# Score products of attention at full array height: a head's high and low query parts stacked in the two row halves

## What is computed

```python
qg = q.reshape(b, T, KV, G, HEAD_DIM)                      # 2 groups of 4 heads
s = jnp.einsum('bcqkgd,bcskd->bckgqs', qc, kw) * SCALE     # window: keys of this and the two chunks before
s = jnp.einsum('bqkgd,bqskd->bqkgs', qg, kg) * SCALE       # sparse: of all earlier keys, the top 256
```

## Time and profile before

| what | us |
|---|---|
| median of 3 runs | 1798.72 (1798.32 to 1801.7) |
| the profiled execution, its own time | 1803.05 |
| span of its instructions | 1801.2 |
| PE busy in the span | 1750.7 (97%) |
| DVE busy | 1257.2 (70%) |
| ACT busy | 726.3 (40%) |
| POOL busy | 588.0 (33%) |

### The profile page before, as it was taken

How to read it: one execution, slowest core, us unless ns; L and a number is a source line. 1 busy time by engine, 2 the same in 40 slices (tenths; PEclk the granted TensorE clock), 3 DMA queues, 4 the chain that set the end, 5 groups by cost and what they waited for, 6 DMA issues and landing times.

```text
span 1801.2 us, 32125 instructions
## 1 busy us (share of the span) xinstructions
PE 1750.7 (97%) x12267; PEld 1700.1 (94%) x12267; DVE 1257.2 (70%) x2174; ACT 726.3 (40%) x1274; POOL 588.0 (33%) x477
## 2 busy tenths in 40 slices
PE   5999999999999999899999999999999999999998
PEld 5999999989999998778889999999999999999998
DVE  5367868978787876688747348866666666776765
ACT  5342122258811123777752335333333333422334
POOL 2211212256634332422231000654555545121030
PEclk9999999999999999999999999999999999999999
DMA  4111111110111112311123210222222222542212
GB/s 147 53 26 52 36 36 53 47 29 25 42 41 52 41 39 78 77 46 38 49 64 116 81 46 26 94 84 72 83 84 72 84 72 75 193 133 81 93 36 97
DMA packets 180435, 121.21 MB, mean 67 GB/s; under 512 B 9340, under 2 KB 165260, under 8 KB 180300
## 3 DMA queue, kind: packets, MB, share of 16 engines
q1 hardware_dynamic: 179324, 117.37, 21.6%
q0 software_dynamic: 976, 2.00, 0.4%
HBM read 101.45 MB, written 17.89 MB: 66 GB/s over the span
## 4 chain that ended last, share of the span: by engine, by line
PE 89%; DVE 5%; ACT 2%; issue 1%; DMA 1%; POOL 1%; SPq 0%; DVEq 0%; ACTq 0%; POOLq 0%
PE ps L1341 36%; PE ps L1711 22%; PE ps L1784 7%; PE ps L1770 6%; PE ps L1353 4%; PE ps L1491 3%; PE ps L1468 3%; PE ps L1606 2%; PE ps L1566 2%; DVE probs L2773 1%; PE ps L1371 1%; DMA w_raw_in_lo<-in_w_in 0%; DMA x_rows<-in_x_prompt 0%; PE ps L1432 0%; PE ps L1433 0%
## 5 line engine op out<-in xcount | busy, mean ns | idle before, releaser
L1079 POOL TENSOR_TENSOR w_lo<-w_raw,w_hi 128x1024 fp32r<-128x1024 f32 (+1 forms) x53 | 100.6, 1897 | 341.6 <-ACT w_hi L1872 341.6
L1341 PE MATMUL ps<-h_hi,w_hi 128*128 128x352 f32 (+1 forms) x912 | 199.6, 327 | 0.0
L1341 PE MATMUL ps<-h_hi,w_lo 128*128 128x352 f32 (+1 forms) x912 | 196.6, 323 | 0.0
L1341 PE MATMUL ps<-h_lo,w_hi 128*128 128x352 f32 (+1 forms) x912 | 196.2, 323 | 0.0
L2587 DVE MAX8 top<-key_mask 128x8 f32<-128x1024 f32 (+5 forms) x176 | 161.5, 920 | 11.3 <-PE ps L1341 1.2
L2587 DVE MATCH_REPLACE8 key_mask<-top,key_mask 128x1024 f32<-128x1024 f32 (+5 forms) x176 | 159.0, 906 | 0.9 <-issue 0.9
L1341 PEld LDWEIGHTS ps<-h_hi,w_lo 128*128 128x128 f32 (+1 forms) x912 | 155.5, 186 | 0.5
L1341 PEld LDWEIGHTS ps<-h_hi,w_hi 128*128 128x128 f32 (+1 forms) x912 | 153.3, 188 | 2.6 <-issue 0.9
L1341 PEld LDWEIGHTS ps<-h_lo,w_hi 128*128 128x128 f32 (+1 forms) x912 | 154.2, 187 | 0.5
L1711 PE MATMUL ps<-mix_hi,quarter_hi 128*128 128x264 f32 x672 | 136.9, 285 | 0.3 <-ACT x_one L1872 0.3
L1711 PE MATMUL ps<-mix_hi,quarter_lo 128*128 128x264 f32 x672 | 136.4, 284 | 0.0
(11 more groups left out here) (364 smaller groups left out, 4580.9 us busy)
## 6 DMA issues: line engine op xcount, KB each, us to landing
w_raw_in_lo<-in_w_in SPq DMA_DIRECT2D x56, 256.0 KB, 2.9
w_raw<-in_w_in SPq DMA_DIRECT2D x54, 256.0 KB, 2.9
ffn_tiles<-t SPq DMA_DIRECT2D x44, 264.0 KB, 2.4
w_raw<-in_w_gate SPq DMA_DIRECT2D x44, 256.0 KB, 3.1
w_raw<-in_w_up SPq DMA_DIRECT2D x44, 256.0 KB, 3.1
w_raw<-in_w_down SPq DMA_DIRECT2D x32, 192.0 KB, 2.7
w_raw_in_lo<-in_w_in SPq DMA_DIRECT2D x44, 128.0 KB, 2.2
ffn<-ffn_tiles SPq DMA_DIRECT2D x20, 264.0 KB, 4.7
```

The lines of the kernel that those rows point to most:

```text
L1079: nc.gpsimd.tensor_tensor(WLO[:, k, 0:tiles, :], raw[:, k, 0:tiles, :], WHI[:, k, 0:tiles, :].bitcast(F32), ALU.subtract).then_inc(lo_read ...
L1341: last = nc.tensor.matmul(PS[0:rows, NB * k + b, 0:e - a], w[:, k, t, 0:rows], x[:, t, a:e], start=m == 0 and w is WHI and x is hi, stop=m ...
```

## The change

A head's high and low query parts now lie in the two row halves of one tensor per head of a job: `Q_EVEN` for h = 0 (high in the lower rows, low in the upper), `Q_ODD` for h = 1 (high in the upper rows, low in the lower). One full-height matmul against `k_hi` gives high by high plus low by high. Up to 512 keys, `k_lo` is taken at full height too (which adds low by low); above 512 keys `k_lo` is taken by halves, as before. A pair of up to 512 keys then has four matmuls of 128 rows in place of six of 64. ACT and DVE write these tensors by halves, two instructions in place of one. The sample queries are copied by DVE from the PSUM banks. PE's waits for `taken` move.

```diff
@@ -288,10 +288,11 @@
         KI_HI = place("idx_k_hi", [P, TOK], F32R, 21)
         KI_LO = place("idx_k_lo", [P, TOK], F32R, 22)
         WIT = place("idx_w", [IDXH, TOK], F32, 23)
-        Q_HI = place("q_hi", [P, NJ, TOK], F32R, 24)
+        Q_EVEN = place("q_parts_even", [P, NJ, TOK], F32R, 24)
         K_LO0 = place("k_lo0", [P, SEQ], F32R, 29)
         K_HI0 = place("k_hi0", [P, SEQ], F32R, 28)
-        Q_LO = place("q_lo", [P, NJ, TOK], F32R, 30)
+        Q_ODD = place("q_parts_odd", [P, NJ, TOK], F32R, 30)
+        Q_PARTS = (Q_EVEN, Q_ODD)
         O_HI = place("attn_hi", [P, NJ, TOK], F32R, 24)
         O_LO = place("attn_lo", [P, NJ, TOK], F32R, 30)
         O_SUM = place("attn_sum", [P, NJ, TOK], F32, 30)
@@ -777,6 +778,10 @@
         def parts_before(pair):
 
             return pair["o"] if pair["window"] else pair["o"] - 1
+
+        def head_bank(k, h):
+
+            return PS[HD * h:HD * (h + 1), NB * k:NB * k + NB, 0:PIECE]
 
         def groups_of(pair):
             return range(NKV) if pair["sample"] else [pair["g"]]
@@ -1542,7 +1547,6 @@
                 pe.wait_ge(rows_out, r_v + 3)
                 if side == 2:
                     fill_sparse(-1, 0)
-                pe.wait_ge(taken[1], n0 // 2 + 3)
 
             def qk(pair):
 
@@ -1558,15 +1562,26 @@
                     return
                 m, at, k0 = 2 * pair["g"] + pair["half"], pair["i"] * P, pair["first"] * P
                 k_hi, k_lo = K_HI[pair["g"]], K_LO[pair["g"]]
+                if pair["i"] == 0:
+                    pe.wait_ge(taken[m % 2], evicted((J_B if pair["window"] else J_C) + 2 + m))
+                if n <= BANK:
+                    for h in range(2):
+                        for k in (k_hi, k_lo):
+                            last = nc.tensor.matmul(scores_of(pair, h), Q_PARTS[h][:, m, at:at + P], k[:, k0:k0 + n],
+                                                    start=k is k_hi, stop=k is k_lo)
+                        last.then_inc(s_done, 1)
+                    return
                 for a in range(0, n, BANK):
                     b = min(a + BANK, n)
-                    for turn, (q, k) in enumerate(((Q_HI, k_hi), (Q_HI, k_lo), (Q_LO, k_hi))):
-                        for h in range(2):
-                            rows = slice(HD * h, HD * (h + 1))
-                            last = nc.tensor.matmul(scores_of(pair, h)[:, a:b], q[rows, m, at:at + P],
-                                                    k[rows, k0 + a:k0 + b], start=turn == 0, stop=turn == 2)
-                            if b == n and turn == 2:
-                                last.then_inc(s_done, 1)
+                    for h in range(2):
+                        nc.tensor.matmul(scores_of(pair, h)[:, a:b], Q_PARTS[h][:, m, at:at + P],
+                                         k_hi[:, k0 + a:k0 + b], start=True, stop=False)
+                    for h in range(2):
+                        rows = slice(HD * h, HD * (h + 1))
+                        last = nc.tensor.matmul(scores_of(pair, h)[:, a:b], Q_PARTS[h][rows, m, at:at + P],
+                                                k_lo[rows, k0 + a:k0 + b], start=False, stop=True)
+                        if b == n:
+                            last.then_inc(s_done, 1)
 
             def pt(pair, c):
 
@@ -1613,6 +1628,7 @@
             def attend_window(ps):
                 for pair in ps[0:2]:
                     qk(pair)
+                pe.wait_ge(taken[1], evicted(J_B + NJ + 1))
                 fill(EARLY_UNITS[1])
                 for y, pair in enumerate(ps):
                     units = units_before(y + 1) - units_before(y)
@@ -1633,6 +1649,7 @@
                 for pair in ps[0:2]:
                     qk(pair)
                 fill_sparse(-1, 1)
+                pe.wait_ge(taken[1], evicted(J_C + NJ + 1))
                 for y, pair in enumerate(ps):
                     late = y + 2 < len(ps) and ps[y + 2]["ahead"] == 1
                     if y + 2 < len(ps) and not late:
@@ -2045,7 +2062,7 @@
                 for g in range(NKV):
                     last = copy(K_HI[g][own[g], :], K_T[own[g], 0:SEQ])
                 last.then_inc(q_hi, 1)
-                act.wait_ge(q_hi, (NJ + 1) * (side - 1) + 1)
+                act.wait_ge(q_hi, (2 * NJ + 1) * (side - 1) + 1)
                 for g in range(NKV):
                     copy(K_HI[g][own[1 - g], :], K_HI[g][own[g], :].bitcast(F32))
                 following(n0, 0, 1, WIN)
@@ -2062,7 +2079,8 @@
                         act.wait_ge(staged, 4 if side == 1 else 6)
                         rows_from(V_ROWS, TRIPLES, r_c + 1 + len(k_tiles), side)
                     done(n0, i, k)
-                    copy(tokens(Q_HI[:, m, :]), group(k)).then_inc(q_hi, 1)
+                    for h in range(2):
+                        copy(tokens(Q_PARTS[h][HD * h:HD * (h + 1), m, :]), head_bank(k, h)).then_inc(q_hi, 1)
 
             def rows_from(dst, tiles, r, side):
 
@@ -2707,20 +2725,21 @@
             def attention_jobs(n0, side, r_v, *work):
 
 
-                heads = (NJ + 1) * (side - 1)
-
-                def sample_queries(g):
-                    for k in range(2):
-                        dve.wait_ge(taken[k], evicted(n0 + 2 + 2 * g + k))
+                heads = (2 * NJ + 1) * (side - 1)
+
+                def low(m, k):
+
                     for h in range(2):
-                        out = QS[HD * g:HD * (g + 1), :].rearrange("p (j t) -> p j t", t=DEC)[:, h:NJ:2, :]
-                        high, lows = (q[HD * h:HD * (h + 1), 2 * g:2 * g + 2, SEQ:TOK].bitcast(F32) for q in (Q_HI, Q_LO))
-                        last = V_.tensor_tensor(out, high, lows, ALU.add)
-                    return last
-
-                def low(n, out, high):
-                    dve.wait_ge(q_hi, heads + n + 1)
-                    V_.tensor_tensor(out, group(k), high.bitcast(F32), ALU.subtract).then_inc(taken[k], 1)
+                        own, other = slice(HD * h, HD * (h + 1)), slice(HD * (1 - h), HD * (2 - h))
+                        j, at = NJ // 2 * (m % 2) + h, SEQ - 2 * PIECE
+                        dve.wait_ge(q_hi, heads + 1 + 2 * m + h + 1)
+                        first = V_.tensor_copy(QS[HD * (m // 2):HD * (m // 2 + 1), j * DEC:(j + 1) * DEC],
+                                               PS[own, NB * k + 2, at:at + DEC])
+                        if (m, h) == (NJ - 1, 1):
+                            first.then_inc(staged, 1)
+                        last = V_.tensor_tensor(tokens(Q_PARTS[h][other, m, :]), head_bank(k, h),
+                                                tokens(Q_PARTS[h][own, m, :]).bitcast(F32), ALU.subtract)
+                    last.then_inc(taken[k], 1)
 
                 for m in range(NJ + 2):
                     k = m % 2
@@ -2739,8 +2758,6 @@
                     if m == NJ + 1 and side == 2:
                         to_mask(SEL[1])
                         to_mask(SEL[2])
-                    if m == NJ + 1:
-                        sample_queries(0)
                     if m == 0:
                         dve.wait_ge(q_hi, heads + 1)
                         dve.wait_ge(lo_ready, n0 + 1)
@@ -2752,9 +2769,7 @@
                             dve.wait_ge(k_lo, NKV * (side - 1) + g + 1)
                             V_.tensor_copy(K_LO[g][own[1 - g], :], K_LO[g][own[g], :].bitcast(F32))
                     elif m > 1:
-                        low(m - 1, tokens(Q_LO[:, m - 2, :]), tokens(Q_HI[:, m - 2, :]))
-
-                sample_queries(1).then_inc(staged, 1)
+                        low(m - 2, k)
 
             def mask_max(pair, h):
```

## The result

The changed kernel takes 1808.72 us in the median (1806.2 to 1809.5, 6 runs). The kernel before, on the same chips, takes 1800.19 (1798.27 to 1801.96, 6 runs), so the ratio is 1.0047, 95% interval 1.0037 to 1.0057: slower by 8.5 us. The forecast was 1801.6 with a range to 1805.5, so the direction was called no change and the size was missed by 7 us. The profiled execution took 1806.2 us, the lowest of its kernel, where the profiled one of before (1803.05) lies above all six of its own. The two traces therefore differ by only 3 us, and the stages have to be compared one by one.

What follows compares the result with a forecast made beforehand. PE was taken to bound the kernel, with 89% of the span on its chain. Terms 2.8 + 0.8 - 0.2 + 2.0 - 5.9 - 1.4 + 4.8 = +2.9 us gave about 1801.6 from the median 1798.72; range 1795.5 to 1805.5.

Steps and rivals of the forecast that it cites:

- The value rows: Side 1: two longer query jobs on DVE make `v_parts` 2.9 us late; PE stands 2.8 us, between 0 and 3.2.
- The start of the window: Side 1, last job: masks start 2.6 us after the first half instead of 1.85; +0.8 us, between 0 and 1.4.
- The clock: Side 1: PE's clock falls to half behind the 2.8 us stop; 2.0 us lost, between 0 and 3.3.
- The window gain: Window stage: 27 pairs at 0.22 us each where PE sets the pace, 5.9 us gained, steps of 3.30 us.
- The price of a pair: Scores of 256 keys: four full-height matmuls without change of height take 0.48 us instead of 0.70; 0.22 gained.
- ACT and DVE at 37 of 44 need 3.52 x 0.84 = 2.96, so they still keep up: Window stage: their work of 2.96 us a step fits in the new step of 3.30 us.
- Up to 512 keys: Sparse stage: shorter pairs on the chain lose their changes of height; 1.4 us gained, between 0 and 2.5.
- above (+4.8): Sparse stage above 512 keys: four height changes a pair, not two; 14 pairs lose 0.34 us each, 0 to 5.4 in all.
- stop for `taken`: PE's moved waits for `taken` were to come when banks are free; a new stop there was a sign against the forecast.
- side 2 cost nothing: Side 2: DVE's extra 0.3 us is hidden, as DVE waits for ACT and PE stands for weights anyway.
- "nothing gained" rivals: Score products: full height doesn't stream (about 1813 us), or 0.34 us belongs to scores as such (1811); chance 0.05 together.
- slower, by the stop at the value rows: Rival: 3.2 us stop in side 1, full clock loss 3.3, all 16 long pairs pay; +5.2, 1804 us, chance 0.30.

Runs made afterwards that it cites:

- e4_grouped: Changed kernel, but above 512 keys the full-height products of all pieces come first, then the products by halves; 1804.28 us, ratio 1.0022.
- e3: Changed kernel's evictions by halves with the score products of the kernel before (three turns by halves, all tiles); 1807.24 us, ratio 1.0039.
- e9: Kernel before, with 8 selection rounds and two masks moved from side 1 to the gate stage behind the window; 1798.99 us, ratio 0.9998.

## Why the prediction was wrong

- **The value rows (2.8 us): right mechanism, a little small.** PE stopped at the place that I named, for the release that I named, 3.32 us. From half to half VectorE takes 1.47 us (352.91 to 354.38), where I had 1.17 + 0.14 = 1.31: neither the low part nor the sample copy (0.19) overlaps its follower. `v_parts` came 3.25 later, not 2.9.
- **The start of the window (0.8): 1.26.** In part for the same reason: 4.91 us to the mask of sample scores against 3.67.
- **The clock (2.0, between 0 and 3.3): 2.4 in the mean, about right.** All six profiled executions with a stop of 3.3 to 3.6 us there fell to the lower clock between 355 and 365. What fell within the stop cost nothing; behind it 2.7 to 2.9 us were lost four times, 1.4 to 1.8 twice (the changed kernel's own is one of the two). The row of e4_grouped from the end of its stop, 10.8 us at 0.74, so 2.8 lost:

```profile
357.20:368.00 10.80, 10.80 (x52) 10.80 (x53) 9.61 (x13) 4.50 (x7) 0.27 (x1) 0.74 0.18 49
```

Side 1 as a whole costs 6.0 to 7.1 us in these six, 6.7 in the mean, where the forecast had 5.4.
- **The window gain (-5.9): this step failed.** It is -3.6. The price of a pair, 0.22 us, was right: with VectorE relieved the stage is 6.0 us shorter than before (118.0 to 112.0). What failed is "ACT and DVE at 37 of 44 need 3.52 x 0.84 = 2.96, so they still keep up". That is a mean over steps. VectorE's steps of before range from 2.51 to 3.38 us, with 3.30 allowed. In the changed kernel nine of the last 24 steps were longer than forecast, by 2.3 us together: four with more than 3.30 us of VectorE's work, five for a reason that isn't shown.
- **Up to 512 keys (-1.4) and above (+4.8): +4.7 to +5.0 net (against e3 and e9) where I had +3.4. The second term was too small.** All 16 long pairs pay, not 14, and 0.34 to 0.41 each, 6.1 us in all; so what is left for the short ones is a gain of 1.1 to 1.4. My upper end of 5.4 was below what came.
- **The base.** I started from 1798.72, a median of three runs; the six beside the result gave 1800.19, 22 later ones 1799.94. That is 1.5 us of the miss of 7.1. Of the other 5.6 the window has 2.3, side 1 has 1.3 and the sparse stage up to 1.6.
- **Not made:** no stop for `taken` appeared in the changed kernel, side 2 cost nothing, full height streams; both "nothing gained" rivals were rightly put low. The rival "slower, by the stop at the value rows" was the true one in side 1, with the stop at its upper price, and it still lacked the window: 6.7 (side 1) - 3.6 + 5.0 = +8.1 us, and measured are 8.5.

## What to carry to other kernels

Cover is read step by step, not as a mean over a stage: take the fullest step of the covering engine against the new, shorter step. That gives the least that is lost: here five steps with less work than that grew too. When a change gives an engine more work, look at what is queued on it there that could be done elsewhere (selection rounds here, 2.7 us each). With the order of the products that turned a loss of 8.5 us into a gain of over 4. Products of different heights belong in blocks of one height; in the pair of 768 keys full height for all was as good as fewer columns (1.87 and 1.86 us), in that of 1024 it was 0.11 us longer.

## What the hardware showed

- A change from 128 to 64 rows and back costs PE 0.34 to 0.42 us, 0.16 to 0.20 for each of the two.
- A small operation of VectorE can last as long as one of GpSimd. The two-column product behind each mask, in the changed kernel:

```profile
456.70 0.95 POOL L1159 TENSOR_TENSOR late_gates<-late_gates,merge_sum 128x352 f32<-128x352 f32 x1
456.90 0.76 DVE L2816 SCALAR_TENSOR_TENSOR softmax_stats<-softmax_stats,sinks_negated 128x2 f32<-128x2 f32 x1
...
460.83 0.16 DVE L2816 SCALAR_TENSOR_TENSOR softmax_stats<-softmax_stats,sinks_negated 128x2 f32<-128x2 f32 x1
```

It takes 0.16 alone and 0.76 beside GpSimd's product, and both end at 457.65. It took 577 ns in the mean of 25 steps of the changed kernel and 515 in the kernel before. The Trainium skill ("SBUF — State Buffer", Who interferes with whom) says that a VectorE instruction with two inputs in SBUF contends with a GpSimd instruction that reads SBUF, and that this is an exclusive lock; the trace agrees, as both end together.
- PE's clock fell to its lower level behind a stop of 3.3 to 3.6 us in side 1 in six executions of six, behind one of 2.33 us in one of six, and behind 1.65 us in none of two, with dense work on both sides each time. At the start of the sparse stage, where a stop of 0.8 to 1.5 us and one of 2.4 to 3.6 stand within 4 us, it fell in all 15 executions. Further on, where two stops of about 1.5 us stand 12 us apart, it fell behind one of them in four of 15.
